# Stick-breaking heads projected first and run between the later projections of their layer, with the output projection taking their rows first

## What is computed

```python
h = rms_norm_2(x, mix_norm_g) * (1.0 + sc_m) + sh_m
dq, dk, dv, sq, sk, sv = jnp.split(h @ w_in, 6, axis=-1)
# 4 differential heads: rope on dq, dk; two softmax maps each; p0 - lam * p1; PV; RMS norm of the output
# 8 stick-breaking heads, causal, s < t:
z = sq @ sk.T * scale
log_1m = where(causal, log_sigmoid(-z), 0)
suffix = reverse_cumsum(log_1m) - log_1m
a = where(causal, exp(log_sigmoid(z) + suffix), 0);  o_sb = a @ sv
x = x + g_m * (concatenate([o_diff, o_sb]) @ w_out)
h = rms_norm_2(x, ffn_norm_g) * (1.0 + sc_f) + sh_f
x = x + g_f * (square(relu(h @ w_ff1)) @ w_ff2)
```

## Time and profile before

| | us |
|---|---|
| median of 3 runs (lowest, highest) | 1879.44 (1878.47, 1880.27) |
| the profiled execution, its own time | 1880.62 |
| its span | 1878.8 |
| busy in the span: TensorE, VectorE, ScalarE, POOL | 1810.1, 1446.6, 1169.2, 197.0 |
| the last layer's projections, 1515.0 to 1589.2 | 74.2 |
| its attention, 1589.2 to 1613.6 | 24.4 |
| its stick-breaking stage, 1613.6 to 1648.0 | 34.4 |
| its output projection, 1648.0 to 1672.2 | 24.2 |

### The profile page before, as it was taken

One profiled execution on the slowest core, in us unless ns is written; L12 is line 12 of the kernel. 1 busy time (PEld: TensorE's weight loads), 2 busy tenths in 40 slices (PEclk: granted clock), 3 DMA queues, 4 the chain that ended last, 5 costly groups with the idle time before them and its releaser, 6 DMA issues.

```text
span 1878.8 us, 27835 instructions
## 1 busy us (share of the span) xinstructions
PE 1810.1 (96%) x10738; PEld 1589.6 (85%) x10738; DVE 1446.6 (77%) x1332; ACT 1169.2 (62%) x1136; POOL 197.0 (10%) x157
## 2 busy tenths in 40 slices
PE   9988999999999999999999999999999999789997
PEld 8977999998878878788787887878877888689997
DVE  6855877779668888888888888888889854765554
ACT  5545444456667777877777778787776744743332
POOL 0032111202020000000000000000006000402221
PEclk9999999999999999999999999999999999999999
DMA  9604798841359999999999999999999933035540
GB/s 393 264 8 168 261 334 321 328 147 44 133 220 385 370 363 380 354 399 379 363 389 355 387 377 367 383 367 385 378 353 414 369 135 136 1 135 182 184 151 23
DMA packets 74572, 520.86 MB, mean 277 GB/s; under 512 B 8064, under 2 KB 8192, under 8 KB 13952
## 3 DMA queue, kind: packets, MB, share of 16 engines
q1 hardware_dynamic: 73056, 514.02, 71.9%
q0 software_dynamic: 1440, 5.77, 0.8%
HBM read 504.02 MB, written 15.73 MB: 277 GB/s over the span
## 4 chain that ended last, share of the span: by engine, by line
PE 85%; DVE 6%; ACT 5%; issue 2%; DMA 1%; POOL 0%; ACTq 0%; DVEq 0%; SPq 0%
PE ps L1185 25%; PE ps L1187 25%; PE ps L1186 25%; DVE wl L1720 2%; ACT wh L1060 1%; PE ps L1402 1%; PE ps L1208 1%; PE ps L1570 1%; DMA raw<-in_experts 1%; PE ps L1331 1%; DVE sqz L1713 1%; PE ps L1352 1%; ACT L1071 0%; ACT L1060 0%; PE ps L1199 0%
## 5 line engine op out<-in xcount | busy, mean ns | idle before, releaser
L1720 DVE TENSOR_TENSOR wl<-raw,wh 128x2048 fp32r<-128x2048 f32 x446 | 1025.0, 2301 | 286.0 <-ACT wh L763 159.4
L1060 ACT ACTIVATE wh<-raw 128x2048 fp32r<-128x2048 f32 x336 | 643.1, 1918 | 181.4 <-PE ps L1187 176.1
L1185 PE MATMUL ps<-wh,xh 128*128 128x512 f32 (+1 forms) x1040 | 398.0, 383 | 10.0 <-DVE wl L1720 10.0
L1187 PE MATMUL ps<-wh,xl 128*128 128x512 f32 (+1 forms) x1040 | 390.1, 375 | 0.0
L1186 PE MATMUL ps<-wl,xh 128*128 128x512 f32 (+1 forms) x1040 | 389.9, 375 | 0.0
L1185 PE MATMUL ps<-xh,wh 128*128 128x256 f32 x1184 | 340.5, 288 | 13.1 <-DVE xl L1720 7.4
L1186 PE MATMUL ps<-xl,wh 128*128 128x256 f32 x1184 | 335.5, 283 | 0.0
L1187 PE MATMUL ps<-xh,wl 128*128 128x256 f32 x1184 | 335.4, 283 | 0.0
L763 ACT ACTIVATE wh<-raw 128x2048 fp32r<-128x2048 f32 x107 | 204.2, 1910 | 173.0 <-PE ps L1187 169.2
L1185 PEld LDWEIGHTS ps<-xh,wh 128*128 128x128 f32 x1184 | 227.7, 192 | 17.7 <-issue 14.8
L1185 PEld LDWEIGHTS ps<-wh,xh 128*128 128x128 f32 x1040 | 195.8, 188 | 51.4 <-DVE wl L1720 17.4
(11 more groups left out here) (302 smaller groups left out, 1957.4 us busy)
## 6 DMA issues: line engine op xcount, KB each, us to landing
raw<-in_experts SPq DMA_DIRECT2D x336, 1024.0 KB, 6.9
raw<-in_units SPq DMA_DIRECT2D x134, 1024.0 KB, 5.7
x_rows<-big SPq DMA_DIRECT2D x1, 6144.0 KB, 35.6
big<-x_rows SPq DMA_DIRECT2D x8, 512.0 KB, 8.2
y_rows<-big SPq DMA_DIRECT2D x7, 512.0 KB, 8.4
y_rows<-big SPq DMA_DIRECT2D x1, 2560.0 KB, 41.5
big<-in_mem SPq DMA_DIRECT2D x1, 1024.0 KB, 7.0
hT<-in_x SPq DMA_DIRECT2D x1, 1024.0 KB, 9.0
```

The costliest lines, as they stand in the source:

```text
L1060: act.activation(wh[:, p % SPL, :], raw[:, n % RAW, :], ACT.Copy).then_inc(sem("hi_ready"), 1)
L1185: mm(out_, lh, rh, start=start, stop=False, **kw)
L1187: return mm(out_, ll, rh, start=False, stop=stop, **kw)
L1720: return V.tensor_tensor(out_, whole, leading.bitcast(F32), ALU.subtract)
```

## The change

The twelve input units come in the order sq0, sk0, sv0, sq1, sk1, sv1, dk0, dk1, dq0, dq1, dv0, dv1, in banks 6 and 7 in turn. TensorE calls `beside(h)` in the middle (h even) and behind (h odd) each of them, which puts scores, suffix sums, outputs and rotations there; the twelve transposes are gone. ScalarE and VectorE have the stick-breaking steps between their drains, splits and ROPE. The outputs' parts go to ah and al, not to xh and xl. Attention comes after that; in its last steps TensorE multiplies wo0's stick-breaking rows and the first sum of the norm. The output projection is in parts: stick-breaking rows of wo0, wo1 and wo2, then the differential rows, then wo3 whole. The differential norm of a pair is in attention's last steps and right behind it. Cut to its core:

```diff
-UNITS_B = ([f"{w}{j}" for w in ("dq", "dk", "dv", "sq", "sk", "sv") for j in range(2)] + [f"wo{j}" for j in range(4)]
+UNITS_B = ([f"{w}{j}" for j in range(2) for w in ("sq", "sk", "sv")] + [f"{w}{j}" for w in ("dk", "dq", "dv")
+           for j in range(2)] + [f"wo{j}" for j in range(4)]
...
-        DIFF_SPLITS = {9: "sv0", 10: "sv1"}
...
-        ROPED = ("dq0", "dq1", "dk0", "dk1")
+        ROPED = ("dk0", "dk1", "dq0", "dq1")
...
-            product(name, (1 + j) % 4)
+        ROT_AT = {14: 0, 17: 1, 19: 2, 21: 3}
...
+        for h in range(2 * len(WIN)):
+            if h % 2 == 0:
+                product(WIN[h // 2], 6 + h // 2 % 2)
+            if h % 4 == 0:
+                for i in pair(h // 4 - 2):
+                    S.add(f"sbx{i}", 2 + i % 2)
+                for i in pair(h // 4 - 1):
+                    S.add(f"sbs{i}", i % 2)
+            if h % 4 == 3 and h >= 11:
+                S.add(f"sbo{h // 4 - 2}", 4, own_signal=True)
+            if h in ROT_AT:
+                S.add(f"rot{ROT_AT[h]}", 5)
+        add_attention(diff_maps)
+        product("wo0", 6)
+        S.add("sub0", 7)
+        product("wo1", 7)
+        S.add("sub1", 4)
+        product("wo2", 0)
+        product("wo3", 1)
...
```

GpSimd: `normalise(diff_maps)`, the scaling of attention's weights, goes behind the masks, and both masks of pair g are in round g. ScalarE:

```diff
+            taken(WIN[0])
+            taken(WIN[1])
+            for g in range(SB_PAIRS + 1):
+                if g >= 1:
+                    sb_weights(g - 1)
+                if g < SB_PAIRS:
+                    sb_logs(g)
+                taken(WIN[2 * g + 2])
+                taken(WIN[2 * g + 3])
+                if g >= 1:
+                    sb_hi(g - 1)
...
+            def sub_first(i):
+                if i == 8:
+                    warm(ACT.Sqrt)
+                elif i == 9:
+                    sub_square(0)
+                elif i == 11:
+                    sub_sd(0)
+
+            attention(diff_maps, sub_first)
+            act.wait_ge(sem("att_pv"), len(maps))
+            sub_square(1)
+            for g in range(DIFF_PAIRS):
+                if g == 2:
+                    sub_sd(1)
+                act.wait_ge(sem("sub_out"), g + 1)
+                act.activation(xh[:, g, :], qT[:, g, :], ACT.Copy).then_inc(sem("sub_hi"), 1)
+
+            wait_done(act, "wo0", nb)
+            split_after("wo0", nb)
```

TensorE:

```diff
-                    if i % 2 == 0:
-                        for _ in range(12):
-                            pe.transpose(x[:, 0:P], ident, ident)
...
+            def beside(h):
+                if h % 4 == 0:
+                    if h >= 8:
+                        sb_suffix(h // 4 - 2)
+                    if 4 <= h < 20:
+                        sb_scores(h // 4 - 1)
+                if h % 4 == 3 and h >= 11:
+                    sb_out(h // 4 - 2)
+                if h in ROT_AT:
+                    r = ROT_AT[h]
+                    wait_drained(pe, ROPED[r])
+                    claim(pe, f"rot{r}")
+                    mm(bank(f"rot{r}"), rot, att_pT[:, r % 2, :], start=True, stop=True).then_inc(filled(f"rot{r}"), 1)
...
+            def beside_diff(i):
+                if i in (8, 9):
+                    wait_drained(pe, f"sbo{SB_PAIRS - 1}")
+                    wo_part("wo0", SB_ROWS, (i - 8,), first=True)
+                elif i == 10:
+                    sub_sum(0)
...
+            attention(diff_maps, beside_diff)
+            wo_part("wo1", SB_ROWS, first=True)
+            sub_sum(1)
+            wo_part("wo2", SB_ROWS, first=True)
+            wo_part("wo0", (0, 1))
+            wo_part("wo0", (2, 3)).then_inc(sem("unit_done"), 1)
+            for name in ("wo1", "wo2"):
+                wo_part(name, DIFF_ROWS).then_inc(sem("unit_done"), 1)
+            wo_part("wo3", (*SB_ROWS, *DIFF_ROWS), first=True).then_inc(sem("unit_done"), 1)
```

VectorE:

```diff
+            split_after(WIN[0], nb)
+            split_after(WIN[1], nb)
+            distances(0)
+            sb_costs(0)
+            split_after(WIN[2], nb)
+            split_after(WIN[3], nb)
+            less_suffix(0)
+            distances(1)
+            sb_costs(1)
+            split_after(WIN[4], nb)
+            split_after(WIN[5], nb)
+            sb_rest(0)
+            less_suffix(1)
+            distances(2)
+            sb_costs(2)
+            split_after(WIN[6], nb)
+            rope(0)
+            split_after(WIN[7], nb)
+            sb_rest(1)
+            less_suffix(2)
+            distances(3)
+            sb_costs(3)
+            rope(1)
+            split_after(WIN[8], nb)
+            split_after(WIN[9], nb)
+            sb_rest(2)
+            rope(2)
+            less_suffix(3)
+            rope(3)
+            split_after(WIN[10], nb)
+            dve.wait_ge(sem("sb_pv"), SBH)
...
+            def beside_diff(i):
+                if i == 0:
+                    sb_rest(SB_PAIRS - 1)
+                elif i == 9:
+                    split_after(WIN[11], nb)
+                elif i == 11:
+                    sub_scale(0)
+
+            attention(diff_maps, beside_diff)
+            sub_scale(1)
+            sub_rest(0)
+            sub_rest(1)
+            sub_scale(2)
+            sub_scale(3)
+            sub_rest(2)
+            sub_rest(3)
```

More of the change, by code:

```diff
@@ L728, in _ @@
             zero_keys(kz, "keys_zeroed")
-            normalise(diff_maps)
             sbm = cc(C_SBM)
-            for g in range(SB_PAIRS + 1):
+            for g in range(SB_PAIRS):
                 for i in pair(g):
@@ L737, in _ @@
                                            ALU.mult).then_inc(sem("sb_masked"), 1)
-                for i in pair(g - 1):
+                for i in pair(g):
                     pool.wait_ge(sem("sb_exp"), i + 1)
@@ L1102, in _ @@
[L1102 to L1113, removed]
@@ L1140, in _, with sb_weights @@
-                if g == 0:
-                    for j in range(2):
-                        wait_filled(act, f"sub{j}")
-                        act.activation(sub_r[:, j, :], bank(f"sub{j}"), ACT.Sqrt, scale=1.0 / P,
-                                       bias=eps).then_inc(drained(f"sub{j}"), 1)
-                for i in pair(g - 1):
+                    act.activation(sb_l[i % 4], sb_l[i % 4], ACT.Ln, bias=1.0).then_inc(sem("sb_log1p"), 1)
+            def sb_weights(g):
+                for i in pair(g):
@@ new lines, in _, with sub_sum @@
+            for j, name in enumerate(WIN):
+                if name[1] == "v":
+                    by_tokens(name, nb, half_done=lambda: beside(2 * j))
+                else:
+                    by_channels(name, nb, arriving("mix2") if j == 0 else None, half_done=lambda: beside(2 * j))
+                beside(2 * j + 1)
+            def sub_sum(j):
+                pe.wait_ge(sem("sub_sq"), j + 1)
+                claim(pe, f"sub{j}")
+                mm(bank(f"sub{j}"), ones, sub_q[:, j, :], start=True, stop=True).then_inc(filled(f"sub{j}"), 1)
@@ new lines, in wo_part @@
+            def wo_part(name, rows, halves=range(2), first=False):
+                h, l = weights(name, KT, nb)
+                if first and halves[0] == 0:
+                    claim(pe, name)
+                for t in halves:
+                    for k in rows:
+                        if k < DIFF_PAIRS:
+                            pe.wait_ge(sem("sub_lo"), k + 1)
+                            x = (xh[:, k, :], xl[:, k, :])
+                        else:
+                            g = k - DIFF_PAIRS
+                            x = [a[:, g // 2, T * (g % 2):T * (g % 2) + T] for a in (ah, al)]
+                        c = slice(P * t, P * t + P)
+                        ins = exact(bank(name)[:, T * t:T * t + T], (h[:, k, c], l[:, k, c]), x,
+                                    first and t == 0 and k == rows[0], k == DIFF_PAIRS - 1, skip_group_check=True)
+                return ins
@@ L2213, in sb_rest, with distances @@
-            def sb_rest(g):
-                dve.wait_ge(sem("sb_hi"), g + 1)
-                rest(xl[:, 4 + g, :], bank(f"sbo{g}")[:, 0:T], xh[:, 4 + g, :]).then_inc(drained(f"sbo{g}"), 1)
-            for i in (*pair(0), *pair(1)):
-                distance(i)
-            for g in range(SB_PAIRS):
+            def distances(g):
+                for i in pair(g):
+                    wait_filled(dve, f"sbs{i}")
+                    if i >= 4:
+                        wait_drained(dve, f"sbs{i - 4}")
+                    z, l = bank(f"sbs{i}")[:, 0:3 * P], sb_l[i % 4]
+                    link(V.tensor_scalar(l, z, -1.0, None, ALU.mult))
+                    V.tensor_tensor(l, z, l, ALU.min).then_inc(sem("sb_abs"), 1)
@@ L2221, in _, with sb_costs @@
+            def sb_costs(g):
                 for i in pair(g):
```

240 lines of the change are left out of this document (97 added, 143 removed).

## The result

The kernel after takes 1864.89 us in the median of four executions (1862.16 to 1866.39); the kernel before, measured beside it, 1879.86 (1878.47 to 1881.99, four). The ratio is 0.9918 with an interval of 0.9901 to 0.9935: 15.0 us less. The profiled execution took 1866.39 us with a span of 1864.6, which is 14.2 under the span of before; the forecast was 17.3.

A forecast was written before the change was run, and what follows sets the result against it. A chain of small stick-breaking steps was taken to bound the kernel, beside engines it could share with the projections. +14.6 + 0.4 + 2.25 - 34.6 = -17.3 us from 1879.44 gives 1862.1 us, range 1859.0 to 1868.5.

The forecast's parts named there:

- rival A: The forecast itself: the whole kernel takes 1862.1 us, with TensorE not waiting in the projections; chance 0.63.
- TensorE's added work: Input projections: scores, suffix sums and outputs of four stick-breaking pairs add 15.5 us of matmuls.
- the walk: Input projections, step by step from the first one's end: attention begins at 82.2 instead of 67.6, +14.6 us.
- the bound of 1 us: Input projections: at most 0.1 us of pipeline refill at each of eleven insertions; the forecast took 0.
- (a): Fifth projection needs the third drained, behind the first pair's logs on ScalarE: ready 17.4, asked 18.6, spare 1.2 us.
- (b): Rotation 0, amid the eighth projection, needs dk0 copied behind the third pair's logs: ready 44.8, asked 45.7, spare 0.9 us.
- 0.4: Attention: VectorE gets one more subtraction of 0.42 us, counted as +0.4 us.
- +2.25: Attention's last four steps: 3.7 us of added TensorE work, less 1.0 and 0.5 in gaps; bounds 0 and 3.7.
- Tail: From the last PV through the output projection: 24.9 us instead of 59.5, so -34.6 us.
- B: Input projections: TensorE waits for ScalarE or POOL's masks, 4 to 6 us in all, say 1867 us; chance 0.20.
- D: More gain: the tail's 2.4 us wait or attention's added time is smaller than counted, 1859.5 us; chance 0.10.
- C: Slower: ScalarE's run from scores to copy exposes the old stage, from about 12.9 us per group; say 1883 us, chance 0.03.

## Why the prediction was right

The forecast of 1862.1 us missed by 2.8, inside its range; rival A is what happened. A miss of 2.8 says little by itself, since three sets of this one program have medians of 1862.8, 1864.9 and 1867.3. The steps say more, with the end of the first product at 1521.70 in the trace after:

**TensorE's added work and the walk.** Attention was to begin at 82.2; it began at 1604.53, which is 82.8. The 0.6 us lie inside the bound of 1 us for eleven insertions. Spare (a) was forecast at 1.2 us: the copy of the third product ended at 1538.51, TensorE asked at 1540.3 by the pace, 1.8. For (a) the forecast listed both table loads of the group; the one for Exp was over (1531.93) in a wait for the distances, so only the one for Ln lies on the path. Spare (b) was forecast at 0.9; it was 0.7. ScalarE's timeline and TensorE's:

```profile
1530.65 1.28 ACT L1124 ACT_TABLE_LOAD   x1
1534.05 0.53 ACT L1124 ACTIVATE big<-big 128x384 f32<-128x384 f32 x1 [2.12 <-DVE big L2277]
...
1535.65 1.28 ACT L1127 ACT_TABLE_LOAD   x1
1536.94 0.94 ACT L1127 ACTIVATE big<-big 128x384 f32<-128x384 f32 x2
1537.91 0.60 ACT L828 ACTIVATE big<-ps 128x512 f32<-128x512 f32 x1
...
1566.09 0.58 ACT L1117 ACTIVATE att_pT<-ps 128x512 f32<-128x512 f32 x1
```

```profile
1567.38 1.02 PE L1715 MATMUL ps<-att_pT,cst 128*128 128x512 f32 x2
```

**The table loads.** The rows just shown decide it: the load for Ln is followed by Ln 1.29 us after its start, with no room for a drain. The rule of the Trainium skill (ScalarE: Activation LUTs, What ACT_TABLE_LOAD costs), 2.66 us a switch, would have made the chain 1.38 us longer at the load for Ln (an estimate); the prediction took it twice, 2.8 us, though the load for Exp lies in a wait. At (a) the spare of 1.8 would have taken that; at (b), with 0.7 and three groups behind it, TensorE would have waited, as it does with the lengthened chain. There is no wait.

**Attention.** Forecast 23.2 + 0.4 + 2.25 = 25.85 us from the first scores to the last PV; 27.6 were measured. At full clock the steps came out: first to last Exp 14.94 us against 15.0, and from the last Exp to the end of the last PV 8.6 us against 6.24 (in the trace before) + 2.25 = 8.5. The missing 1.7 is the granted clock. The +2.25 was partly luck. TensorE was busy without a gap there, as forecast; but POOL's scaling, held for 2.1 us by the split, ran beside it and is in no term. Where the rows were gone it took their place, so of 2.25 us only 0.6 could be had back.

**Tail.** First scaling done at 2.3, measured 2.5; scaling 2 started at 6.1, measured 6.1; last scaling done at 10.5, measured 10.55; rests at 11.4, measured 11.5; TensorE's wait 2.4, measured 2.0. The last product was to end at 24.0 and ended at 25.7; in the execution at full clock that part is 1.5 us shorter, 24.2. One step of the tail did fail, and in the kernel's favour: ScalarE was to square the last residual 0.9 us late, behind the split of a1, and I put that on the path. At full clock the square is indeed late, its start just at the end of that split:

```profile
1653.34 1.90 ACT L765 ACTIVATE wh<-raw 128x2048 fp32r<-128x2048 f32 x1
1655.14 0.61 ACT L782 ACTIVATE sqz<-hT 128x512 f32<-128x512 f32 x1
```

But the reciprocal comes 2.4 us behind the start of that square and 3.05 behind the one of the trace after, which was not held up. What sets it is TensorE, whose sixteen sums take 3.62 us from the end of the last product, and the other rows' come first (VectorE, in a split until 1657.55, would not have been free sooner either). So the delay was covered, and 0.9 us too much stood in the sum.

Together 0.6 + 1.7 + 1.7 - 0.9 = 3.1 over the forecast, the 3.1 us by which the span's 14.2 falls short of 17.3. **The term that was mis-sized is the one that wasn't there: the granted clock.** The prediction wrote that steady work leaves no stretch at the lower level, and counted that as a chance of more gain. Between the projections that held in every trace of this kernel (behind the first 4 us in one). But TensorE went from those into attention's small waits, where the clock can fall, and fell in some executions. The execution in which it held everywhere had a stage 17.2 us shorter than before, against 17.3; there the late start of 0.6 and the tail's 0.2 stand against the 0.9 that was covered.

**The rivals.** B did not happen in the kernel after. D did not either: at full clock the gain is the forecast's, not more. Nor did C, and its point of take-over, 12.9 us a group, was not tried. The chain 3 us longer per group gave back 8.8 us: lateness carries over from group to group, and what the last asker's spare does not take is waited for. An estimate by the same count, with 5.4 us more in each of three groups: 16.2 - 0.7 = 15.5 us and the clock on top, near the 17.3 that C needs. What was wrong was the 3 us expected of the long chain, which set each place's spare against one group's lateness alone.

## What to carry to other kernels

When a chain of small steps is laid beside long products, walk every in-order queue to the point where the product asks, and carry the lateness on: spares of 1 us were right to 0.6 us or better here, but three groups lengthened by 3 us cost 8.8 us, not the 3 that each place by itself would let through. Find the rows of a later product whose inputs are early and put them over the serial chain in front of it; about half of the gain here depends on that. Before work is moved off a place, ask what it covered: a POOL instruction held for 2.1 us appeared on the path only once wo0's rows had gone. Compare kernels by the stage that changed, with the clock of each part beside it: here the same program's stage differs by up to 3.1 us.

## What had not been expected of the hardware

TensorE's clock falls or holds in the same program at the same place. With equal waits (0.18, 0.65, 1.41 us) it was at 1.2 GHz from 1612 to 1616 in one execution and at 2.4 GHz all through in the other. Three places of this stage showed it, at prices that came back in most traces: start of the projections 1.2 to 1.3 us, attention 0.8 or 1.7 to 1.8, output projection 1.5. What decides between the cases within one program was not found. Of six traces with attention's waits left open the clock held there in one (1.00); with filler or real work in them it held in all three. That work is the cause is likely by this, not shown. Filler cost as much there (1.5 us) as the fall; real work cost 0.1.
